# At three joints of a decoder trunk, GpSimd makes the next projection's first four low weight parts instead of VectorE

## The reference

```
h = rmsnorm(x, g_pre_mix[l]) * (1.0 + sc1) + sh1
y = hybrid_mixer(h, ...)          # h @ w_in, then mLSTM, S5 and sparse attention heads, then y @ w_out
x = x + gt1 * rmsnorm(y, g_post_mix[l])
h = rmsnorm(x, g_pre_ffn[l]) * (1.0 + sc2) + sh2
y = conv_ffn(h, ...)              # h @ w_up, gated with a causal convolution of width 3, then @ w_down
x = x + gt2 * rmsnorm(y, g_post_ffn[l])
```

## Time and profile before

| | us |
|---|---|
| runs of before | 2635.11, 2619.44, 2626.44 |
| median | 2626.44 |
| profiled execution, whole | 2627.05 |
| its span, first to last instruction | 2625.2 |
| PE busy | 2418.4 (92%) |
| VectorE (DVE) busy | 1981.8 (75%) |
| ScalarE (ACT) busy | 1290.4 (49%) |
| GpSimd (POOL) busy | 292.9 (11%) |
| mean granted TensorE clock | 0.975 |

### The profile page before, as it was taken

The page is one execution under the profiler, slowest core; times in us unless marked ns, Lnnn a source line. Parts: engine busy times, 40 slices in busy tenths (PEclk is TensorE's granted clock), DMA queues, the critical chain, the costliest instruction groups (busy, mean ns, idle before and its releaser), DMA issues.

```text
span 2625.2 us, 41113 instructions
## 1 busy us (share of the span) xinstructions
PE 2418.4 (92%) x14368; PEld 2130.6 (81%) x14368; DVE 1981.8 (75%) x2448; ACT 1290.4 (49%) x2051; POOL 292.9 (11%) x434
## 2 busy tenths in 40 slices
PE   1499989988999999999998999998899999999998
PEld 1499978767888888878888998886688888887886
DVE  8898888788999999856668978765698666665555
ACT  1365456445444444444447446554544554554444
POOL 1031321111111112101001212000010000000000
PEclk9999989999999999999999999999999999999999
DMA  9758877676999888867764686644387555555654
GB/s 396 274 183 277 310 255 250 216 307 219 331 330 335 326 314 321 333 214 270 273 247 157 234 280 249 183 179 165 122 320 276 190 188 190 189 188 172 195 192 152
DMA packets 193004, 643.13 MB, mean 245 GB/s; under 512 B 28480, under 2 KB 38736, under 8 KB 190960
## 3 DMA queue, kind: packets, MB, share of 16 engines
q1 hardware_dynamic: 125056, 455.96, 49.4%
q0 software_dynamic: 47216, 170.80, 18.7%
q10 hardware_dynamic: 20608, 14.72, 1.8%
HBM read 626.68 MB, written 14.71 MB: 244 GB/s over the span
## 4 chain that ended last, share of the span: by engine, by line
PE 68%; DVE 20%; ACT 4%; issue 4%; DMA 3%; POOL 0%; DVEq 0%; ACTq 0%; POOLq 0%
PE ps L1110 21%; PE ps L659 17%; PE ps L1111 10%; PE ps L644 7%; DVE ada_acc L1591 6%; DVE w_lo L1585 5%; PE ps L984 4%; DVE mix L1585 3%; ACT w_hi L1172 2%; DMA ring<-stream 1%; PE ps L602 1%; DVE mix L1591 1%; PE ps L629 1%; PE ps L776 1%; DVE mix L1588 1%
## 5 line engine op out<-in xcount | busy, mean ns | idle before, releaser
L1585 DVE TENSOR_TENSOR w_lo<-ring,w_hi 128x1024 fp32r<-128x1024 f32 x744 | 914.3, 1233 | 535.8 <-ACT w_hi L1172 534.3
L1172 ACT ACTIVATE w_hi<-ring 128x1024 fp32r<-128x1024 f32 x744 | 786.8, 1058 | 913.4 <-PE ps L1111 333.8
L1110 PE MATMUL ps<-hT,w_hi 128*128 128x512 f32 x2688 | 938.6, 395 | 4.5 <-DVE w_lo L1585 4.4
L1111 PE MATMUL ps<-hT,w_lo 128*128 128x256 f32 x2688 | 747.9, 278 | 0.0
L1110 PEld LDWEIGHTS ps<-hT,w_hi 128*128 128x128 f32 x2688 | 504.1, 188 | 124.8 <-DVE w_lo L1585 5.4
L1111 PEld LDWEIGHTS ps<-hT,w_lo 128*128 128x128 f32 x2688 | 505.8, 188 | 0.0
L644 PE MATMUL ps<-hT,w_hi 128*128 128x256 f32 x2496 | 476.1, 293 | 9.3 <-DVE w_lo L1585 9.3
L1591 DVE SCALAR_TENSOR_TENSOR ada_acc<-ada_w,cs,ada_acc 128x1024 f32<-128x1024 f32 x348 | 445.9, 1282 | 16.3 <-DMA ada_w<-ada_d 3.9
L644 PEld LDWEIGHTS ps<-hT,w_hi 128*128 128x128 f32 x2496 | 402.5, 198 | 15.8 <-issue 15.2
L644 PE MATMUL ps<-hT,w_lo 128*128 128x256 f32 x1248 | 359.7, 288 | 0.0
L644 PEld LDWEIGHTS ps<-hT,w_lo 128*128 128x128 f32 x1248 | 246.5, 198 | 0.0
(11 more groups left out here) (264 smaller groups left out, 2467.9 us busy)
## 6 DMA issues: line engine op xcount, KB each, us to landing
ring<-stream SPq DMA_DIRECT2D x760, 512.0 KB, 4.3
ada_w<-ada_d POOLq DMA_DIRECT2D x320, 512.0 KB, 5.5
ring<-ada_d SPq DMA_DIRECT2D x36, 512.0 KB, 9.6
ada_w<-ada_d SPq DMA_DIRECT2D x28, 512.0 KB, 9.8
xs<-x SPq DMA_DIRECT2D x2, 2048.0 KB, 11.4
s_in_w<-mix ACTq DMA_DIRECT2D x8, 512.0 KB, 3.8
s_out_w<-mix ACTq DMA_DIRECT2D x16, 256.0 KB, 5.5
ring<-s_in_w SPq DMA_DIRECT2D x8, 512.0 KB, 6.6
```

The lines of the kernel that those rows point to most:

```text
L1110: pe.matmul(ps[:, bank, :], w_hi[:, s, ks], hT[:, k, :, :], start=k == 0, stop=False)
L1111: m = pe.matmul(ps[:, bank, SEQ:2 * SEQ], w_lo[:, s, ks], hT_hi[:, k, :], start=False, stop=k == KT - 1)
L1172: s.activation(w_hi[:, c % SPLIT, :], ring[:, at % RING, :], ACT.Copy).then_inc(hi_ready, 1)
L1585: return v.tensor_tensor(o, a, b, op)
```

## The change

The diff in full:

```diff
@@ GpSimd, in the loop over layers @@
+                def splits(n):
+
+                    wait(raw_free, n)
+                    for k in range(SPLIT):
+                        wait(hi_ready, n + k + 1)
+                        pool.tensor_tensor(w_lo[:, (n + k) % SPLIT, :], ring[:, ring_place((n + k) % NS) % RING, :],
+                                           w_hi[:, (n + k) % SPLIT, :].bitcast(F32), ALU.subtract).then_inc(raw_free, 1)
+
                 for a in range(N_OUT[l]):
                     unit(U_OUT[l] + a, a, U_OUT[l] + a - 1)
+                splits(l * NS + S_UP)
                 for i in range(N_UP[l]):
                     unit(U_UP[l] + i, 0, U_UP[l] + i)
                 for a in range(N_DOWN[l]):
...
                     pool.dma_start(aux[:, :], aux_d[l + 1, :, :]).then_inc(aux_in, 16)
+                    splits((l + 1) * NS)
@@ VectorE @@
                 def norm_in(n, c):
                     modA_ready.wait(v, l, n + 1)
                     for b in range(8):
-                        if b == 2:
+                        if b == 2 and not (n or l):
                             w_rest(c + 3)
...
+                    if n or l:
+                        v.wait_ge(raw_free, l * NS + c + SPLIT)
...
                 def joint(n, l, c, units, at, gain):
 
                     residual(n, 0)
-                    w_rest(c, l=l)
                     residual(n, 1)
...
                     norm_gain((n + 1) % 2, gain, l)
-                    w_rest(c + 1, l=l)
                     scaled((n + 1) % 2, 1, l)
-                    w_rest(c + 2, l=l)
```

## The result

| | before | changed |
|---|---|---|
| median of 5 runs each, us | 2632.81 | 2649.14 |
| lowest to highest | 2619.44 to 2644.49 | 2642.44 to 2653.11 |
| profiled execution's span | 2625.2 | 2640.6 |
| GpSimd (POOL) busy | 292.9 | 330.4 |
| VectorE (DVE) busy | 1981.8 | 1987.8 |

The changed kernel takes 1.0057 of the time of before, 95% interval 1.0033 to 1.0081: slower, +15 us, where 2641 against 2626 (+0.56%) was forecast. With all five runs the median of before is 2632.81 us and not 2626.44, so it is the differences that can be compared: the medians differ by 16.3 us, the two spans by 15.4, and the forecast was 14.8.

The account below looks back on a forecast made before the run. VectorE's queue was taken as the critical path up to the transposes at three joints, TensorE being 92% busy; net costs 4.6 + 5.0 + 5.2 = 14.8 us took the 2626.44 us median to 2641, range 2629 to 2661.

Parts of the forecast that it names:

- What the removal gives: At each joint, low parts leaving VectorE: first 1.14 us, fourth 0.7, two hidden ones nothing; 1.8 us, 5.5 at most.
- The norm_in term: Fourth low part, in norm_in: without it TensorE's steps run at their own pace, saving 0.7 us per joint, bounds 0 and 1.14.
- the first term: First low part, between the residuals at each joint: its removal takes 1.14 us off VectorE's path to the transposes.
- The length: GpSimd subtraction of 128x1024: holds VectorE back 2.3 us; floor 1.3 us, upper bound without surprise 2.6, ceiling 4.6.
- Who is held: At the joints, GpSimd's subtraction holds VectorE's residual and scaling, about 2.3 us each, but not the gate, which reads PSUM.
- the second rival: Partial hold: scaling parts pass before GpSimd's third or fourth subtraction, or are not held; 2629 to 2635 us, chance 0.17.
- Which comes first: Start order of GpSimd's first subtraction and VectorE's first residual; at joint 2 either order, differing by 0.2 us, GpSimd assumed first.
- The transfers behind: Next unit's MEMSET, bias row and first four ada_w transfers, queued behind GpSimd's subtractions: no cost beyond the MEMSET's 0.8 us.
- the term, 5.3 us: Joint 3: first pair of t = 1 transposed, and ScalarE's first hT row begun, 5.3 us later than before.
- The rival of a longer subtraction: At 4.6 us per GpSimd subtraction, from its fp32r result, the holds add 27.6 us: 2669 us, chance 0.13.
- that of no loss: VectorE is not held, or the subtractions fall into its gate and PSUM work: 2621 us, chance 0.08.

Follow-up runs that it names:

- the write-only work: Changed kernel, each of GpSimd's twelve subtractions replaced by a MEMSET of 1024 unused columns, those low parts left out; joints 31.46, 33.12 and 28.85 us.

## Why the prediction was right

The mechanism, the sign and the size held: 14.8 us forecast, 13.4 us in the joints. That the span's 15.4 us lie nearer to the forecast is chance: 2.0 of them are outside the joints. Some of the agreement in the joints is luck too, since two errors went against each other. By its steps:

- **What the removal gives.** 1.8 us per joint at most was said, 5.5 in all; the kernel without the subtractions shows 1.6, 1.2 and 2.0, in all 4.8, with the moved MEMSET counted in. The norm_in term, 0.7, measured 0.6 to 0.7. At joint 2 the first term was too large: the gate of t = 1 then waits 0.56 us for ScalarE, so 0.6 us are gained and not 1.14.
- **The length.** 2.3 us of hold and at least 2.4 of duration were taken; alone a subtraction takes 2.34 us and the fp32r result costs nothing extra: half the width takes 1.26 us, what fp32 took in the earlier trace rows. A residual that came 0.11 us late was held 2.04 us, so the hold is 2.15 us; the two holds among joint 2's scaling parts make 5.54 - 1.68 = 3.86 us, 1.9 each. This is the mis-sized term. Counted from the gate, VectorE ended the scaling of t = 0 after 16.64, 17.34 and 16.88 us at joints 1, 2 and 3, where the working had 17.27, 18.35 and 17.71: 2.5 us too much in all, some 0.5 us at each joint in the third and fourth hold and most of the rest in what comes before them at joints 2 and 3.
- **Who is held.** Said: the residual yes, the gate no, the scaling yes. All three are in the rows of joint 3 above, and the write-only work split the rule: a MEMSET does not hold the residual, and it does hold the scaling. The short operations did not keep their turn before GpSimd's third and fourth subtraction, which rules out the second rival. But the turns were not all as worked out: at joints 1 and 2 each side went once and let the other in, at joint 3 the MEMSET followed the fourth subtraction at once and the second scaling part waited for both (3.45 us).
- **Which comes first.** Joint 2 was left open within 0.2 us: the residual won by 0.11 us and kept 2.35. VectorE was through with the second residual 11.57 us after the gate, against 12.05 in the working, which had put GpSimd first and the difference at 0.2.
- **The transfers behind.** Costed at nothing but the MEMSET. VectorE's idle time before its modulation steps grew from 16.3 to 17.0 us over the whole program, and nothing of the loss is left once the subtractions are out. TensorE never waited for a low part from GpSimd.
- **A point missed in the working.** At joint 3 TensorE could start after one scaling part and began its transposes 3.2 us late but reached the first pair of t = 1 5.6 us late. The working had it done with t = 0 as the parts came; in truth it had 12 of the 16 transposes of t = 0 still ahead at 1896.83, and its granted clock stayed at 0.50 for some 6 us there instead of 5.4. I had not priced that. It took back 1.1 us: VectorE was 0.8 us ahead of the working, yet the term, 5.3 us, came out at 5.6. The sign that TensorE's idle time ahead of the first transpose grows by 4 to 6 us held at joint 2 alone: it grew by 2.1, 5.1 and 3.2 us, and at joint 1 the rest lies ahead of the reductions that come first.

The rival of a longer subtraction and that of no loss are out.

## What to carry to other kernels

An idle GpSimd is not free hands for VectorE. Here the same subtraction took 2.34 us on GpSimd and 1.22 on VectorE, and while it ran it held VectorE's operations with two SBUF inputs (2.35 us became 4.39); its writes alone also held the one-input fp32 operation from SBUF to SBUF. Put such work only beside VectorE operations that read PSUM or beside its waits, and look at who starts first. Before moving work off an engine, ask which of its steps are on the path: here two of the four were hidden, and better places on VectorE itself, without a second engine, shortened the joints by 2.2 us in all, too little to be seen in the times.

## What the runs showed of the hardware that I had not expected

TensorE's granted clock can fall back within a few us of having risen. It did in nine of the joints profiled, always soon after the new projection's first matmuls: joints 1 and 3 of the three kernels that moved the first low part there, and all three of the kernel with the third and fourth held back. It then stayed at 0.50 for some 3 us. In the other twenty-seven of the 36 it stayed at 1.00. What the rows show of the difference: in the nine, TensorE began its first matmul 7.45 to 8.93 us after the first transpose, and its clock had come back 2.5 to 4.5 us after that transpose. In twenty-five of the others the first matmul came after 6.66 to 7.30 us; in the last two, joint 3 of the changed kernel and of the half-width one, it came after 9.6 and 8.6 us, and the clock had come back only after 6 us or more. What a fall costs can be read from kernels with the same place of the fourth low part, from VectorE's first row in norm_in on: 0.7 to 0.8 us with the fourth before block 2, where the steps wait for VectorE, and 1.2 to 1.4 us with it before block 5, where they wait less. Eight more transposes in the gap did not prevent it. What decides is open.
